# A hybrid decoder step on one core: the entry to the 32 experts reordered

## The reference, cut to what matters

```
logits = xt @ w_router + b_router
top_val, top_idx = top_k(logits, 4);  w_top = softmax(top_val)
combine = sum over k of w_top[:, k] * one_hot(top_idx[:, k], 32)
for e in range(32):
    a = xt @ w_gate_up[e] + b_gate_up[e]                  # 1024 -> 2 x 1024
    gate = min(a[:, :1024], 7);  up = clip(a[:, 1024:], -7, 7)
    h = (up + 1) * gate * sigmoid(1.702 * gate)
    out += combine[:, e] * (h @ w_down[e] + b_down[e])    # 1024 -> 1024
```

## Time and profile before

| | us |
|---|---|
| median of 3 runs (1358.86 to 1361.56) | 1360.79 |
| the profiled execution | 1358.12 |
| its span, first to last instruction | 1356.3 |
| TensorE busy in the span | 1304.1 (96%) |
| VectorE, ScalarE, GpSimd busy | 364.0, 253.4, 101.4 |
| bytes moved | 499.03 MB, mean 368 GB/s |
| dense trunk, up to the first expert's product | 0 to 441 |
| experts | 441 to 1345 |
| last norm and stores | 1345 to 1356 |

### The profile page before, as it was taken

How to read it: one execution, slowest core, us unless ns; L and a number is a source line. 1 busy time by engine, 2 the same in 40 slices (tenths; PEclk the granted TensorE clock), 3 DMA queues, 4 the chain that set the end, 5 groups by cost and what they waited for, 6 DMA issues and landing times.

```text
span 1356.3 us, 17073 instructions
## 1 busy us (share of the span) xinstructions
PE 1304.1 (96%) x6899; PEld 692.5 (51%) x6899; DVE 364.0 (27%) x796; ACT 253.4 (19%) x566; POOL 101.4 (7%) x133
## 2 busy tenths in 40 slices
PE   9999999999999999999998998989999998998988
PEld 7848887788887344344243433424434343342433
DVE  3864433211456222113021111202212112120212
ACT  4314345221125111011110101101011011010102
POOL 2652221001200000000000000000000000000000
PEclk9999999999999999999999989999999999999999
DMA  9894567548969999999999999999999999999996
GB/s 325 285 363 156 202 242 246 197 145 309 293 234 377 389 417 426 429 428 429 428 429 429 429 428 428 428 429 423 430 428 430 427 430 428 431 427 428 430 425 263
DMA packets 64898, 499.03 MB, mean 368 GB/s; under 512 B 5967, under 2 KB 7352, under 8 KB 39768
## 3 DMA queue, kind: packets, MB, share of 16 engines
q1 hardware_dynamic: 51424, 453.37, 81.1%
q0 software_dynamic: 13216, 44.50, 9.7%
q10 hardware_dynamic: 216, 0.58, 0.1%
HBM read 491.34 MB, written 7.08 MB: 367 GB/s over the span
## 4 chain that ended last, share of the span: by engine, by line
PE 75%; DMA 20%; DVE 1%; POOL 1%; issue 1%; SPq 0%; ACT 0%; ACTq 0%; DVEq 0%; POOLq 0%
PE bank L1348 22%; PE bank L804 17%; PE bank L1368 13%; DMA arena<-in_w_down 10%; DMA ring<-in_w_gate_up 9%; PE bank L1401 4%; PE bank L1332 4%; PE bank L754 1%; PE bank L1357 1%; PE bank L838 1%; PE bank L1363 1%; PE bank L1285 1%; PE bank L1182 1%; PE bank L767 1%; DMA ring<-in_cache_kv_latent,arena 1%
## 5 line engine op out<-in xcount | busy, mean ns | idle before, releaser
L1348 PE MATMUL bank<-ring,arena 128*64 128x512 f32 x1536 | 344.8, 597 | 6.4 <-DMA ring<-in_w_gate_up 6.4
L1368 PE MATMUL bank<-arena 128*64 128x512 f32 x1000 | 229.3, 609 | 30.2 <-DMA arena<-in_w_down 30.2
L804 PE MATMUL bank<-arena,ring 128*128 128x264 f32 x1008 | 230.7, 388 | 0.0
L1348 PEld LDWEIGHTS bank<-ring,arena 128*64 128x64 f32 x1536 | 104.3, 137 | 222.4 <-issue 206.9
L804 PEld LDWEIGHTS bank<-arena,ring 128*128 128x128 f32 x1008 | 189.4, 190 | 36.0 <-issue 4.4
L1368 PEld LDWEIGHTS bank<-arena 128*64 128x64 f32 x1000 | 70.4, 140 | 173.9 <-issue 129.0
L2607 DVE TENSOR_TENSOR resid<-resid,bank 128x264 f32<-128x264 f32 x128 | 54.8, 429 | 355.0 <-PE bank L1401 353.5
L1348 PE MATMUL bank<-arena 128*64 128x512 f32 x512 | 115.5, 593 | 3.5 <-DMA arena<-in_w_gate_up 3.5
L2612 DVE TENSOR_SCALAR arena<-bank 128x512 f32<-128x512 f32 x32 | 22.0, 688 | 340.8 <-PE bank L1348 340.8
L1566 ACT ACTIVATE arena<-bank 128x264 f32<-128x264 f32 (+6 forms) x129 | 51.0, 403 | 165.9 <-PE bank L804 126.8
L1946 ACT COPY arena<-bank 64x512 f32<-64x512 f32 x63 | 36.5, 580 | 232.9 <-PE bank L1368 232.1
(11 more groups left out here) (364 smaller groups left out, 933.2 us busy)
## 6 DMA issues: line engine op xcount, KB each, us to landing
ring<-in_w_gate_up SPq DMA_DIRECT2D x94, 2048.0 KB, 28.9
arena<-in_w_down SPq DMA_DIRECT2D x62, 2048.0 KB, 22.2
arena<-in_w_gate_up SPq DMA_DIRECT2D x32, 2048.0 KB, 28.8
ring<-in_w_in SPq DMA_DIRECT2D x10, 2048.0 KB, 11.4
out<-arena POOLq DMA_DIRECT2D x8, 512.0 KB, 5.0
ring<-v_rows POOLq DMA_DIRECT2D x8, 512.0 KB, 6.0
ring<-in_w_o_mla SPq DMA_DIRECT2D x2, 2048.0 KB, 8.9
ring<-in_w_o_gla SPq DMA_DIRECT2D x2, 2048.0 KB, 15.2
```

Of the source, the lines that this page charges most:

```text
L804: mm = nc.tensor.matmul(lin_bank(name)[0:m, 0:width], w(ring_name, nk, cols)[:, k, a:a + m], rhs[:, k, 0:width], start=(k == 0), stop=(k = ...
L1348: mm = nc.tensor.matmul(B[i // 2][CAP * (i % 2):CAP * (i % 2) + CAP, :], xg[:, k, CAP * e:CAP * e + CAP], slot(n)[:, a:a + 512], start=Fal ...
L1368: mm = nc.tensor.matmul(bank[CAP * half:CAP * half + CAP, :], hidden[:, k % 4, CAP * (k // 4):CAP * (k // 4) + CAP], weights[:, 512 * half ...
```

## The change

Seven edits, all between the router and the end of the first pair:

1. The order of the row tiles (`ROWS`): the two tiles of the samples come last, and the three matmuls for the ranks stand ahead of the sixth tile.
2. VectorE starts `posm` right after `take`, makes the one-hots ahead of a copy, and no longer clears `wselT`.
3. The first gather is cut: `gather_first` gathers two row chunks for the first expert alone; `gather_second` gathers the rest after two rows of the first expert's product. ACT's Exp for the router's softmax comes after the first copy of seats.
4. The reload of slot 2 is cut into halves like those of slots 3 and 1.
5. `b_down` is loaded four times, column block c of each half into row group c (four loads of 512 B pieces instead of one of 4 KB rows), and `combine` is turned into all four row groups (`turn_choices`), after six rows of the first expert instead of after four.
6. The bias of the down product is scattered from 32 rows each, in the row group c % 4 (`scatter_down_biases`), in groups of 3, 3 and 2 matmuls instead of 3, 2 and 3 on 128 rows.
7. In the first pair the first half of the down product stands ahead of the gather of the second pair, not behind it.

```
-        ROWS = [(tt, g) for g in range(2) for tt in range(3)]
+        ROWS = [(0, 0), (1, 0), (0, 1), (1, 1), (2, 0), (2, 1)]
...
-                    for j in range(2):
+                    for j in range(3):
                         n = GATE_UP_SLOT[j][0]
                         first_half, second_half = (slot(n)[:, 2 * DFF * c:2 * DFF * c + 2 * DFF][:, None, :] for c in range(2))
                         sp.wait_ge(S("first_row_used"), j + 1)
                         sp.dma_start(first_half, gate_up_of(2, j)[:, 0:1, :]).then_inc(S(f"slot{n}_loaded"), 16)
                         sp.wait_ge(S(f"slot{n}_used"), 1)
                         sp.dma_start(second_half, gate_up_of(2, j)[:, 1:2, :]).then_inc(S(f"slot{n}_loaded"), 16)
-                    load_gate_up(2, 0, 1, 2, 4)
+                    load_gate_up(2, 0, 1, 3, 4)
...
-            pool.dma_start(y_rows[0:32, :], b_down[0]).then_inc(S("biases"), 16)
             for j in range(4):
+                pool.dma_start(y_rows[32 * j:32 * j + 32, :].rearrange("p (h c n) -> p h c n", h=2, c=4)[:, :, j, :],
+                               b_down[0].rearrange("e (h c n) -> e h c n", h=2, c=4)[:, :, j, :]).then_inc(S("biases"), 16)
                 pool.dma_start(b_gu[32 * j:32 * j + 32, :], b_gate_up[0, :, 512 * j:512 * j + 512]).then_inc(S("biases"), 16)
...
-            for i in range(6):
+            for i in range(5):
                 turn_row_tile(i)
...
             nc.tensor.matmul(ranks[:, 0:3 * NE], ones, take_wide[:, 0:3 * NE], start=True, stop=False)
             nc.tensor.matmul(ranks[:, 0:2 * NE], con("before"), take_wide[:, NE:3 * NE], start=False, stop=False)
             nc.tensor.matmul(ranks[:, 2 * NE:3 * NE], ones, take[:, 0, :], start=False, stop=True).then_inc(S("product_full"), 1)
+            turn_row_tile(5)
...
+            def gather_first():
+                for k in range(2):
+                    for tt in range(2):
+                        mm = nc.tensor.matmul(B[3][:, P * k:P * k + CAP], hn_tok[:, tt, P * k:P * k + P], sel[:, tt, 0:CAP], start=(tt == 0), stop=(tt == 1))
+                mm.then_inc(S("gathered"), 1)
+
+            def gather_second():
+                for k in range(4):
+                    first = CAP if k < 2 else 0
+                    for tt in range(2):
+                        mm = nc.tensor.matmul(B[6][:, P * k + first:P * k + P], hn_tok[:, tt, P * k:P * k + P], sel[:, tt, first:P], start=(tt == 0), stop=(tt == 1))
+                mm.then_inc(S("gathered"), 1)
...
-                    elif k in (0, 2) and e == 0 and isinstance(p, int) and isinstance(q, int) and q == 0:
+                    elif k in (0, 2, 4) and e == 0 and isinstance(p, int) and isinstance(q, int) and q == 0:
                         mm.then_inc(S("first_row_used"), 1)
...
+            def scatter_down_biases(first, last):
+
+                turned(pe, "cwt")
+                for c in range(first, last):
+                    if c >= 3:
+                        pe.wait_ge(S("added"), c - 2)
+                    rows = slice(32 * (c % 4), 32 * (c % 4) + 32)
+                    nc.tensor.matmul(B[5 + c % 3][:, 0:T], y_rows[rows, 128 * c:128 * c + 128], wselT[rows, :], start=True, stop=True)\
+                        .then_inc(S("scattered"), 1)
+
+            def turn_choices():
+                for tt, (t0, n) in enumerate(TILES):
+                    for j in range(4):
+                        mm = nc.tensor.matmul(turn_bank("cwt")[32 * j:32 * j + 32, t0:t0 + n], cw[0:n, tt, 0:NE], ident[0:n, 0:n], start=True, stop=True)
+                mm.then_inc(S("turn_full"), 1)
...
                     gate_up_rows(0, 2, 0, p, q)
+                    gather_second()
                     gather(1, 0, 2)
                     pe.wait_ge(S("x_pair"), 2)
                     gate_up_rows(2, 4, 0, p, q)
+                    lin_done(pe, "rk")
                     gather(1, 2, 4, B[2])
...
                 if first and isinstance(m, int):
-                    pe.wait_ge(S("routed"), 1)
-                    turn("cwt", [(t0, cw[0:n, tt, 0:32]) for tt, (t0, n) in enumerate(TILES)])
-                if first and isinstance(m, int):
                     pe.wait_ge(S("x_pair"), 3)
                     gate_up_rows(4, 6, 0, p, q)
+                    assert TURN[order[1]] == "cwt"
+                    order[1] += 1
+                    pe.wait_ge(turn_sem("cwt"), TI["cwt"] // 2)
+                    pe.wait_ge(S("routed"), 1)
+                    turn_choices()
                     pe.wait_ge(S("x_pair"), 4)
                     gate_up_rows(6, KC, 0, p, q)
...
                 if at_beginning:
-                    turned(pe, "cwt")
-                    scatter(m, 0, 3)
+                    scatter_down_biases(0, 3)
                 banks_clipped(n + 1)
                 bias_rows(1)
                 gate_up_rows(0, 4, 1, p, q)
                 turn_hidden(n)
-                scatter(m, 3 if at_beginning else 0, 5)
+                if at_beginning:
+                    scatter_down_biases(3, 6)
+                else:
+                    scatter(m, 0, 5)
                 gate_up_rows(4, KC, 1, p, q)
-                scatter(m, 5, KC)
+                if at_beginning:
+                    scatter_down_biases(6, KC)
+                    down_half(0, n, p, 2 * q)
+                else:
+                    scatter(m, 5, KC)
 
                 pe.wait_ge(S("selected"), m + 2)
                 gather(0)
                 pe.wait_ge(S("added"), 8 * m + 8)
                 gather(1)
                 turn_weights(m)
-                down_rows(n, p, 2 * q)
+                if not at_beginning:
+                    down_half(0, n, p, 2 * q)
+                down_half(1, n, p, 2 * q)
...
-            pe.wait_ge(S("biases"), 80)
+            pe.wait_ge(S("biases"), 128)
             pe.wait_ge(S("bias_picked"), 1)
             bias_rows(0)
             pe.wait_ge(S("rows_copied"), 6)
             for k in range(KC):
                 mm = nc.tensor.transpose(B[4][:, 64 + SAMPLE * k:64 + SAMPLE * k + SAMPLE], hn_tok[0:SAMPLE, 2, P * k:P * k + P], ident[0:SAMPLE, 0:SAMPLE])
             mm.then_inc(S("rows_turned"), 1)
-            lin_done(pe, "rk")
             pe.wait_ge(S("selected"), 1)
-            gather(0, 0, 2)
-            gather(0, 2, 4, B[6])
+            gather_first()
...
-            act.wait_ge(S("top_shifted"), 1)
-            nc.scalar.activation(weights, weights, ACT.Exp).then_inc(S("top_exp"), 1)
...
                     act.wait_ge(S("gathered"), 1)
-                    seats_out(0, 0, 2)
+                    nc.scalar.copy(xg[:, 0:2, 0:SEATS], B[3][:, 0:2 * P].rearrange("p (k c) -> p k c", k=2)[:, :, 0:SEATS]).then_inc(S("x_pair"), 1)
+                    act.wait_ge(S("top_shifted"), 1)
+                    nc.scalar.activation(weights, weights, ACT.Exp).then_inc(S("top_exp"), 1)
                     act.wait_ge(S("gathered"), 2)
+                    nc.scalar.copy(xg[:, 0:2, CAP:CAP + SEATS], B[6][:, 0:2 * P].rearrange("p (k c) -> p k c", k=2)[:, :, CAP:CAP + SEATS])
                     seats_out(0, 2, 4, B[6])
...
             V.tensor_tensor(take, unpicked[:, :, PADS:], logits[:, :, PADS:], ALU.not_equal).then_inc(S("taken"), 1)
-            V.memset(wselT, 0.0).then_inc(S("weights_copied"), 1)
+            dve.wait_ge(S("taken"), 1)
+            link(V.tensor_scalar(posm[:, 0:2, 0:NE], take[:, 0:2, :], -FAR, FAR, ALU.mult, ALU.add))
             V.tensor_tensor(weights, logits[:, :, PADS:], bc(top8[:, :, 0:1], [P, 3, NE]), ALU.subtract).then_inc(S("top_shifted"), 1)
...
             pick_bias(eyes[:, 0:2])
-            dve.wait_ge(S("taken"), 1)
-            link(V.tensor_scalar(posm[:, 0:2, 0:NE], take[:, 0:2, :], -FAR, FAR, ALU.mult, ALU.add))
             lin_full(dve, "rk")
             link(V.tensor_tensor(posm[:, 0:2, 0:NE], posm[:, 0:2, 0:NE], lin_bank("rk")[:, 0:2 * NE].rearrange("p (t e) -> p t e", t=2), ALU.add))
+            one_hots(posm[:, :, 0:2])
             V.tensor_copy(cnts[:, 0:NE], lin_bank("rk")[:, 2 * NE:3 * NE]).then_inc(S("product_out"), 1)
-
-            one_hots(posm[:, :, 0:2])
```

More of the change, by code:

```diff
@@ L1337, in earlier_loads @@
                 at_beginning = isinstance(p, int) and isinstance(q, int) and q == 0
-                return RING_SLOT.count(n) + (1 if n in (3, 1) and not at_beginning else 0)
+                return RING_SLOT.count(n) + (1 if n in (3, 1, 2) and not at_beginning else 0)
             def gate_up_rows(first, last, e, p, q):
@@ L1396, in scatter @@
                 pe.wait_ge(S("y_rows"), 4 * m + 4)
-                pe.wait_ge(S("weights_copied"), m + 1)
+                pe.wait_ge(S("weights_copied"), m)
                 for c in range(first, last):
@@ L1486, in last_expert @@
                 rows_of_residual(0)
-                pe.wait_ge(S("weights_copied"), m + 2)
+                pe.wait_ge(S("weights_copied"), m + 1)
                 rows_of_residual(2)
@@ L1529, in _ @@
                 pe.wait_ge(S("y_rows"), 2 * NE + 4)
```

(4 more changed lines are left out.)

7 lines of the change are left out of this document (2 added, 5 removed).

## The result

The changed kernel takes 1360.92 us (median of 20 runs, 1359.66 to 1366.31), the kernel before, beside it, 1359.15 (20 runs, 1357.55 to 1362.52). The ratio is 1.0016, with a 95% interval of 1.0009 to 1.0023 (the two medians alone give 1.0013): 1.2 to 3.1 us slower. The forecast was 0.7 us faster. The profiled execution takes 1359.7 us (span 1357.8) against 1358.12.

What follows compares the result with a forecast made beforehand. The weight stream (428 GB/s) was taken to set the time; the hole at 485 closes and the rest cancels, -0.7 us, so the median 1360.8 becomes 1360.1. Own range 1358.9 to 1361.3, with the far cases 1357.0 to 1363.5.

Steps and rivals of the forecast that it cites:

- slot 9's first load: Entry: waits for the sixth row tile, now behind the ranks; issued about 0.45 us later (bounds 0.2 and 0.7), a loss.
- TensorE waiting behind the first scatter: First scatter group: shorter scatter buys nothing, as the next bias waits for both clips; TensorE goes on 1.5 us behind slot 6.
- slot 8: Early down half: starts at 477.1, takes 3.55 us, so slot 8 is free at 480.7 instead of 484.98.
- the hole at 485: Stream at 485 to 490, 360 GB/s where slot 8's reload is issued, 0.8 us lost; forecast to close.
- the law of the stream: Weight loads: each 2 MB load lands at the later of 4.9 us behind the one ahead and 7.7 us behind its issue.
- Here every shift up to then, good or bad, ends: Slot 4's reload: lands at 472.75, before 472.7, so earlier shifts cancel and TensorE's release decides.
- TensorE is late at slot 4: Rival: narrow gathers and turned choices run one by one, slot 4 free at 468.5; +2.7 us, 1363.5; chance 0.08.
- The sum: Stream through the entry: slot 9's reload lands at 497.25 instead of 498.0, -0.7 us.
- the choices: Turned choices on TensorE: 24 instructions on four column groups take 0.45 us (bounds 0.3 and 3.3).
- Release of slot 4: End of TensorE's chain through the entry: slot 4 released at 465.0, 1.1 us later than 463.90.
- the halves: Six 1 MB half loads in the entry: 2.87 us each at 365 GB/s, the last landing at 462.5.
- The gain of 0.7 us: Whole change: slot 9's reload lands 0.7 us sooner because the hole at 485 closes, the rest cancelling.

Runs made afterwards that it cites:

- b1: The changed kernel unaltered, run again as a control and for a second profile; ratio to the kernel before 1.0011 [0.9999, 1.0022].
- b3: The kernel before with one edit alone, slot 2 reloaded in two halves (three halved loads); ratio to the kernel before 0.9999 [0.9988, 1.0010].
- a1: The kernel before with only the first pair's early down half (edit 7); ratio to the kernel before 0.9993 [0.9984, 1.0003].
- d2: The kernel before with only the early down half, a second time; ratio to the kernel before 1.0005 [0.9996, 1.0014].
- d4: The changed kernel with the first down half back behind the second gather; ratio to the kernel before 1.0015 [1.0006, 1.0024].

## Why the prediction was wrong

What bounds the kernel was right, and so were most of its steps. In forecast and trace: slot 9's first load 0.45 later, 0.56; first product at 440.2, 440.43; second at 446.7, 446.95; TensorE waiting behind the first scatter until both clips end, 0.83 us of it in the trace; slot 8 sooner than its 484.98, at 480.7, and 481.75; the hole at 485 closed, 433 GB/s.

**The failed step is the law of the stream**: "a load lands at the later of 4.9 us behind the one ahead, and 7.7 us behind its issue". It was read from loads that met an empty queue and from loads far ahead, with nothing in between, and it makes a lead of 2.8 us enough. Slot 4's reload had 2.9 and landed 7.4 us behind the one ahead, 10.3 behind its issue. In b1, the second profile of the changed kernel, it landed 4.9 us behind the one ahead, as the law has it; there slot 6's reload, asked for 4.0 us ahead, had landed 5.7 us behind the last half. Counted from slot 0's issue, slot 4's reload landed at 45.9 and at 44.1, where the forecast makes it 42.6 (472.75 - 430.13). So the sentence that rested on the law fails too: "Here every shift up to then, good or bad, ends". The shifts did not end there but passed on into slot 4's landing, and the limit of the rival "TensorE is late at slot 4", 465.8, was set as if there were a microsecond to spare. The release came at 465.74, inside that limit, and the time was longer all the same. This rival held the right mechanism at the wrong price; it had 0.08 of the chance.

The trace of the kernel before already spoke against the law. Slot 6's reload, issued at 457.74, was asked for 4.3 us ahead of the landing in front, and yet it landed 5.6 us behind that landing and 9.9 us behind its issue. Applied to the kernel before from 462.0 on, the law puts slot 9's reload at 497.6 and not at the measured 498.0. The sum set a landing by the law against a measured one, so 0.4 of its 0.7 us was an error of the law and no gain.

The forecast time, 1360.1, lies close to the measured 1360.92, and that is luck. It was laid on the median of three runs of the kernel before, 1360.79, which 20 runs put at 1359.15; the gain that was forecast came out as a loss.

**Second, TensorE's terms were a little small, all in one direction.** `gather_first` was put at 0.105 us an instruction and took 0.129; `gather_second` took 1.98 instead of 1.85; the choices 0.75 instead of 0.45. The row behind the first of these, 0.66 / 6 for "one column and full weights", mixes two forms: two of its six instructions load 8 columns of weights and not 128. The groups of TensorE's instructions by line and shape in the changed kernel, 400 to 500 (behind the bar the busy time in us, the mean of one in ns, and the idle time ahead), show the reason:

```profile
L1336 PE MATMUL bank<-arena 128*128 128x128 f32 x8 | 1.1, 282 | 0.0
L1329 PE MATMUL bank<-arena 128*128 128x64 f32 x8 | 1.1, 281 | 0.0
L1429 PE MATMUL bank<-consts_sb,arena 128*32 128x128 f32 x16 | 0.6, 279 | 0.0
```

The mean of one (neighbours overlap) is the same for 64 columns as for 128. Cutting the gather therefore only adds eight instructions. Release of slot 4: 0.74 later than forecast.

**Third, the halves.** Six of them from 445.4 to 463.4 take 3.0 us each, 349 GB/s, not 2.87. By "DMA: Bandwidth & Descriptors" of the Trainium skill, section Bandwidth (341 GB/s for 1 MB), the six take 18.45 us, an estimate; measured 18.0. With it the sum had been 0.0, nearer but not there. That the halves cost time by themselves is neither shown nor excluded: b3, with three pairs of them and nothing else, is at 0.9999, and the fit over twelve kernels leaves -0.2 to 1.3 us for the third pair.

**The gain of 0.7 us** for the hole at 485 rested on the same law. The hole closes in the trace, but a1, d2 and d4 show no gain that the runs can tell.

What stays open: why a load with a lead of 2 to 5 us sometimes loses nothing and sometimes 2.5 us (the changed kernel's two profiles have spacings of 7.4 and 4.9 at the same release), and how much each of the parts other than the split gather adds, the third halved load above all; their shares are below the 0.1% that these runs can tell.

## What to carry to other kernels

Where a stream of loads sets the time, look at how long each load is asked for ahead of the landing in front of it, over all loads of the trace, before calling a later release free: what counts is the lead at which the spacing of the landings starts to grow, here about 8 us, and not the latency of a load into an empty queue. Work on an engine that is off the critical path on average still costs most of its time where it stands ahead of a buffer's release with a short lead (here 0.86 us of each microsecond). Cutting a matmul into narrower ones pays only if narrow ones are cheaper: look for a row with that width first.

## What the runs showed of the hardware

- An instruction of a float32 matmul (two to a matmul) with 128 x 128 weights takes 0.129 us in a row of eight with 64 columns (1.03 / 8, L1329 in the changed kernel) and 0.124 in a row of 16 with 128 (1.98 / 16, L1332 in the kernel before).
- Three scatter products on 32 rows each, in different row groups, take 0.65 us (six instructions, at 469.81) where those on 128 rows took 1.53; the 24 small instructions of the turned choices, on column groups, take 0.75.
- In the changed kernel the six 1 MB halves, each asked for 3 to 6 us ahead of the landing in front, land 2.4 to 4.5 us apart, 3.0 in the mean, while the engines are busy for a share of 0.97 (the window at 446).
